# Norms of memory, cross-attention and first feed-forward: raw rows turned and split inside the preceding product, root mean square applied at eviction

## What is computed

```
mem_h = rms_norm(mem, mem_norm_g)
x = x + hybrid_mixer(rms_norm(x, mix_norm_g), ...)            # ends with @ w_mix_out
x = x + memory_cross_attention(rms_norm(x, xa_norm_g), mem_h, w_xq, w_xkv, w_xo)
x = x + conv_glu_ffn(rms_norm(x, ffn_norm_g), w_gate, w_up, ffn_conv_w, ffn_conv_b, w_down)
x = rms_norm(x, final_norm_g)

def rms_norm(x, g):
    return x * rsqrt(mean(x * x, axis=-1) + EPS) * g

def memory_cross_attention(h, mem_h, w_xq, w_xkv, w_xo):
    q = h @ w_xq
    kv = mem_h @ w_xkv          # keys: columns 0 to 2047, values: 2048 to 4095
    ...                          # 4 heads of 512, softmax over the 256 rows of memory
    return o @ w_xo
```

## Time and profile before

| | |
|---|---|
| median of 3 runs | 3050.98 us (3050.21 to 3056.83) |
| the profiled execution's own time | 3051.17 us |
| its span, first to last instruction | 3049.4 us |
| granted TensorE clock, mean | 0.961 of full speed |
| TensorE matmul busy | 2847.0 us, 93% |
| VectorE busy | 1822.8 us, 60% |
| ScalarE busy | 1300.3 us, 43% |
| moved by DMA | 579.27 MB, mean 190 GB/s |

### The profile page before, as it was taken

The page is one execution under the profiler, slowest core; times in us unless marked ns, Lnnn a source line. Parts: engine busy times, 40 slices in busy tenths (PEclk is TensorE's granted clock), DMA queues, the critical chain, the costliest instruction groups (busy, mean ns, idle before and its releaser), DMA issues.

```text
span 3049.4 us, 36718 instructions
## 1 busy us (share of the span) xinstructions
PE 2847.0 (93%) x13510; PEld 2411.1 (79%) x13510; DVE 1822.8 (60%) x2029; ACT 1300.3 (43%) x1519; POOL 181.1 (6%) x135
## 2 busy tenths in 40 slices
PE   7997899998988999999999979988888999999997
PEld 7996787787877888888888769777677888888885
DVE  6776647766747655544555477865466444444454
ACT  4444323444434555533444344334444434344442
POOL 0001440000000000000000000920000000000000
PEclk9998899999999999999999989988899999999998
DMA  8893008686838455555555558761273555555552
GB/s 292 294 322 106 0 28 289 240 282 209 280 106 275 147 184 179 179 193 187 185 179 193 176 209 298 234 233 56 71 260 112 195 189 180 192 193 180 193 180 97
DMA packets 291579, 579.27 MB, mean 190 GB/s; under 512 B 9040, under 2 KB 46064, under 8 KB 289936
## 3 DMA queue, kind: packets, MB, share of 16 engines
q1 hardware_dynamic: 289920, 565.03, 55.3%
q0 software_dynamic: 1552, 12.76, 1.1%
HBM read 575.66 MB, written 2.10 MB: 189 GB/s over the span
## 4 chain that ended last, share of the span: by engine, by line
PE 86%; DVE 8%; ACT 3%; issue 2%; DMA 1%; POOL 0%; DVEq 0%; SPq 0%; ACTq 0%; POOLq 0%
PE GP L812 25%; PE GP L814 25%; PE GP L813 25%; PE TA L788 2%; PE TB L439 2%; PE TB L788 1%; DVE wlo L1498 1%; DVE ada_acc L1486 1%; PE TA L1103 1%; DMA raw<-in_w_in 1%; PE GP L425 1%; ACT whi L1174 1%; DVE flat L1574 1%; PE GP L788 0%; PE TB L829 0%
## 5 line engine op out<-in xcount | busy, mean ns | idle before, releaser
L1498 DVE TENSOR_TENSOR wlo<-raw,whi 128x1024 fp32r<-128x1024 f32 (+2 forms) x904 | 1082.1, 1215 | 820.1 <-ACT whi L1174 808.3
L1174 ACT CAST whi<-raw 128x1024 fp32r<-128x1024 f32 (+2 forms) x904 | 921.4, 1030 | 1219.8 <-PE GP L814 1168.5
L812 PE MATMUL GP<-whi,hhi 128*128 128x512 f32 (+2 forms) x2752 | 1067.2, 388 | 30.1 <-DVE wlo L1498 26.8
L813 PE MATMUL GP<-wlo,hhi 128*128 128x512 f32 (+2 forms) x2752 | 1058.5, 385 | 0.0
L814 PE MATMUL GP<-whi,hlo 128*128 128x512 f32 (+2 forms) x2752 | 1058.2, 385 | 0.0
L812 PEld LDWEIGHTS GP<-whi,hhi 128*128 128x128 f32 x2752 | 520.5, 189 | 123.5 <-DVE wlo L1498 22.5
L814 PEld LDWEIGHTS GP<-whi,hlo 128*128 128x128 f32 x2752 | 519.9, 189 | 89.6
L813 PEld LDWEIGHTS GP<-wlo,hhi 128*128 128x128 f32 x2752 | 520.3, 189 | 88.0 <-issue 1.0
L1486 DVE SCALAR_TENSOR_TENSOR ada_acc<-raw,csig,ada_acc 128x512 f32<-128x512 f32 x360 | 284.6, 790 | 10.2
L812 PE MATMUL GP<-whi,f2hi 128*128 128x512 f32 x512 | 204.7, 400 | 0.0
L814 PE MATMUL GP<-whi,f2lo 128*128 128x512 f32 x512 | 202.8, 396 | 0.0
(11 more groups left out here) (370 smaller groups left out, 1899.2 us busy)
## 6 DMA issues: line engine op xcount, KB each, us to landing
raw<-in_w_up SPq DMA_DIRECT2D x108, 1024.0 KB, 5.2
raw<-in_w_down SPq DMA_DIRECT2D x108, 1024.0 KB, 5.1
raw<-in_w_ada SPq DMA_DIRECT2D x96, 1024.0 KB, 5.1
raw<-in_w_gate SPq DMA_DIRECT2D x44, 1024.0 KB, 5.1
raw<-in_w_in SPq DMA_DIRECT2D x48, 856.0 KB, 5.0
raw<-in_w_xkv SPq DMA_DIRECT2D x32, 1024.0 KB, 5.3
raw<-in_w_in SPq DMA_DIRECT2D x24, 1024.0 KB, 5.1
raw<-in_w_in SPq DMA_DIRECT2D x24, 864.0 KB, 4.8
```

What stands on the lines that cost most here:

```text
L812: pe.matmul(o, ahi[:, kt, t], whi[r][:, k, 0:q.width], start=first, stop=False)
L813: pe.matmul(o, ahi[:, kt, t], wlo[r][:, k, 0:q.width], start=False, stop=False)
L1174: nc.scalar.copy(whi[(2 * g + s) % NRING][:, :, 0:q.width], raw[j % NSLOT][:, 2 * s:2 * s + 2, 0:q.width])\
L1498: TTo(wlo[r][:, :, 0:q.width], raw[j % NSLOT][:, 2 * s:2 * s + 2, 0:q.width], whi[r][:, :, 0:q.width].bitcast(F32), ALU.subtract).then_inc ...
```

## The change

Rows are turned as they are, without the root mean square, and that factor is applied later, to the product's rows when they are evicted; it is the same for a whole row, so it may be moved behind the product. The gain, which belongs to columns, is applied when the turned columns are split. The steps:

- TensorE: `raw_turn(s, k)` turns 2 of the 16 groups of 128 columns (4 transposes) into one bank of `TA`. s = 0 is the memory, in mix_out; s = 1 is x, in xkvb; s = 2 is x again, in xo (k = 0 to 5) and in the first iteration of ffn1a (k = 6 and 7). xkv is now two phases, xkva with the keys and xkvb with the values.
- ScalarE: `raw_square` squares and sums the rows, `raw_root` takes the root of both halves of the tokens at once, `raw_upper` makes the upper part straight from PSUM, scaled by the gain.
- VectorE: `raw_mean`, `raw_scale` (the reciprocal) and `raw_lower`.
- Evictions of xkva, xkvb, xq, ffn1a and ffn1b: two scaled copies of 512 columns in place of one copy of 1024.
- The keys are turned inside xq (`key_turn`, 8 transposes behind each of its first four units) and copied there (`key_copy`).
- xkvb, xq, xo and mix_out have their last iteration written out, ffn1a its first.
- The split of x for the feed-forward goes to new tiles `bhi`, `blo`; `fhi` moves to the place of `hhi` and `hlo`. `fgb` lies where `bhi` and `blo` are, so POOL waits for ffn1b in place of down1b.

```diff
-          Phase("xkv", 4, 2, 4, 512, True), Phase("xq", 2, 2, 4, 512, True),
+          Phase("xkva", 2, 2, 4, 512, True), Phase("xkvb", 2, 2, 4, 512, True), Phase("xq", 2, 2, 4, 512, True),
...
+        def spot(v):
+
+            return (v // 8, v % 8 + 1) if v % 8 >= LEAD else (v // 8 - 1, v % 8 + 9)
...
             for e in range(2):
-                g.wait_ge(S(f"evac{e}"), 1 + PH["down1b"].ev1)
-            g.wait_ge(S("f1_lo"), 12)
+                g.wait_ge(S(f"evac{e}"), 1 + PH["ffn1b"].ev1)
             g.dma_start(fgb[:, :], A["final_norm_g"].partition_broadcast(P)).then_inc(S("fgb_in"), 16)
...
+            def raw_turn(s, k):
+                n = 8 * s + k
+                X = raws[s][0]
...
+                if n >= 2:
+                    pe.wait_ge(S("raw_lo"), n - 1)
+                for j in range(2):
+                    for h in range(NH):
+                        m = turn(raw_bank(n)[:, j * T + h * P:j * T + h * P + P], X[:, h, (2 * k + j) * P:(2 * k + j + 1) * P])
+                m.then_inc(S("raw_t"), 1)
...
-                    first=lambda: None, points={(0, 0, 1): dn_turn})
-            pe.wait_ge(S("evac1"), 1 + PH["mix_out"].ev1)
-            norm("mem")
-            product(PH["xkv"], hhi, hlo, lambda u: N("mem", "lo", 2 * u + 2))
-            for e in range(2):
-                pe.wait_ge(S(f"evac{e}"), 1 + PH["xkv"].ev1)
-            pe.wait_ge(S("ada_read"), 1 + PH["xkv"].ada1)
-            turn_in(pe, turn, "kx", kv, 0, 0)
-            norm("xa")
-            product(PH["xq"], hhi, hlo, lambda u: N("xa", "lo", 2 * u + 2))
+                    first=lambda: None, points={(0, 0, 1): dn_turn} | {unit_of(6 + k): lambda k=k: raw_turn(0, k) for k in range(8)})
+            product(PH["xkva"], mhi, mlo, lambda u: (S("raw_lo"), 2 * u + 2))
+            product(PH["xkvb"], mhi, mlo, lambda u: (S("raw_lo"), 8),
+                    first=lambda: None, points={unit_of(2 * k): lambda k=k: raw_turn(1, k) for k in range(8)})
...
+            product(PH["xq"], hhi, hlo, lambda u: (S("raw_lo"), 8 + 2 * u + 2),
+                    first=lambda: pe.wait_ge(S("raw_lo"), 16), points={unit_of(k): lambda k=k: key_turn(k) for k in range(4)})
...
-            product(PH["xo"], hhi, hlo, lambda u: N("xatt", "lo", 8))
-            norm("ffn")
+            product(PH["xo"], hhi, hlo, lambda u: N("xatt", "lo", 8), first=lambda: None,
+                    points={unit_of(v_): lambda k=k: raw_turn(2, k) for k, v_ in enumerate((6, 7, 10, 11, 14, 15))})
...
+            rest = product(PH["ffn1a"], bhi, blo, lambda u: (S("raw_lo"), 16 + 2 * u + 2), ffn1_mid(ba), ffn1_end(ba),
+                           points={(0, 0, 1): lambda: (raw_turn(2, 6), raw_turn(2, 7))})
...
+            def raw_upper(s, k):
+                n = 8 * s + k
+                act.wait_ge(S("raw_t"), n + 1)
+                _, g_, hi, _ = raws[s]
+                for j in range(2):
+                    m = nc.scalar.activation(hi[:, 2 * k + j, :], raw_bank(n)[:, j * T:j * T + T], ACT.Copy, scale=gains[:, g_, 2 * k + j:2 * k + j + 1])
+                m.then_inc(S("raw_hi"), 1)
...
+                            for h in range(NH):
+                                m = nc.scalar.activation(dst[:, h, bass.ds(col, q.width)], GP[:, 2 * e + h, 0:q.width], ACT.Copy,
+                                                         scale=scale_of[scale][:, h:h + 1])
...
+            phase(PH["mix_out"], hooked({6: lambda: raw_square(0, (0,)), 7: lambda: raw_square(0, (1,)), 11: lambda: raw_root(0)},
+                                        hooked(uppers(0, range(8, 16)))), peel=True)
+            phase(PH["xkva"], store(PH["xkva"], kv, scale=0))
+            phase(PH["xkvb"], hooked({3: lambda: raw_square(1, (0,)), 5: lambda: raw_square(1, (1,)), 9: lambda: raw_root(1)},
+                                     hooked(uppers(1, range(2, 18, 2)), store(PH["xkvb"], kv, base=2048, scale=0))), peel=True)
...
+            phase(PH["ffn1a"], ffn1(PH["ffn1a"], 0), head={3: [lambda it: raw_square(2)],
+                                                           4: [lambda it: (raw_upper(2, 6), raw_upper(2, 7), raw_root(2))]})
...
+            def raw_lower(s, k):
+                n = 8 * s + k
+                dve.wait_ge(S("raw_hi"), n + 1)
...
+                    m = nc.vector.scalar_tensor_tensor(lo[:, 2 * k + j, :], raw_bank(n)[:, j * T:j * T + T], gains[:, g_, 2 * k + j:2 * k + j + 1],
+                                                       hi[:, 2 * k + j, :].bitcast(F32), ALU.mult, ALU.subtract)
```

More of the change, by code:

```diff
@@ L211, in program @@
         STAGES, grown = {}, dict.fromkeys(("ss", "ms", "rt", "xn", "t", "f", "hi", "lo"), 0)
[L212 removed]
+        for n in ("mix", "fin", "pre2", "post0", "pf2", "post1"):
             STAGES[n] = ("norm", dict(grown))
@@ L601, in turn_in2_act, with raw_bank, hooked @@
                 m = nc.scalar.copy(dst[:, a:a + 4, :], v((TA, TB)[g % 2], T)).then_inc(N(nm_, "c")[0], 1)
[L603 to L606, removed]
+        xn_of = {"mix": xn, "pre2": xn_f, "pf2": None}
+        raws = [(memt, 2, mhi, mlo), (x, 1, hhi, hlo), (x, 3, bhi, blo)]
+        def raw_bank(n):
+            return TA[:, 512 * (n % 2):512 * (n % 2) + 512]
+        def spot(v):
+            return (v // 8, v % 8 + 1) if v % 8 >= LEAD else (v // 8 - 1, v % 8 + 9)
+        def hooked(table, more={}):
+            out = {at: list(fs) for at, fs in more.items()}
+            for v_, f in table.items():
+                t_, at = spot(v_)
+                out.setdefault(at, []).append(lambda it, t_=t_, f=f: f() if it == t_ else None)
+            return out
         ar = Arena(); ar.at = arena0 + 4 * NH * D
@@ L1193, in body, with phase @@
                         f(it)
-            def phase(q, hooks, peel=False, last={}, ahead=True):
+            def phase(q, hooks, peel=False, last={}, ahead=True, head={}):
                 i0 = order.index(q)
@@ L1200, in phase @@
                 m = q.n if same else q.n - 1
-                if m:
+                if head:
+                    body(q, 0, (q, 1), {at: hooks.get(at, []) + head.get(at, []) for at in hooks.keys() | head.keys()})
+                    with loop(act, m - 1) as i:
+                        body(q, i + 1, (q, i + 2), hooks)
+                elif m:
                     with loop(act, m) as it:
@@ L1519, in body, with phase @@
                     nc.vector.tensor_copy(mod[:, bass.ds(4 * (it + q.ada0), 4)], TB[:, 512:516]).then_inc(S("ada_read"), 1)
-            def phase(q, hooks, peel=False, links=0, last={}, ahead=True):
+            def phase(q, hooks, peel=False, links=0, last={}, ahead=True, head={}):
                 i0 = order.index(q)
@@ L1526, in phase @@
                 m = q.n if same else q.n - 1
-                if m:
+                if head:
+                    body(q, 0, (q, 1), {at: hooks.get(at, []) + head.get(at, []) for at in hooks.keys() | head.keys()})
+                    with loop(dve, m - 1) as i:
+                        with link.loop(i, m - 1, per):
+                            body(q, i + 1, (q, i + 2), hooks)
+                elif m:
                     with loop(dve, m) as it:
@@ L1742, in _ @@
                 TTo(hlo[:, 8:16, t], AB[0][hf], hhi[:, 8:16, t].bitcast(F32), ALU.subtract).then_inc(S("dn_lo"), 1)
-            phase(PH["mix_out"], add_to_x(PH["mix_out"]))
-            dve.wait_ge(S("mem_in"), 16)
-            norm("mem", memt, gains[:, 2, :])
-            phase(PH["xkv"], {})
-            norm("xa", x, gains[:, 1, :])
+            phase(PH["mix_out"], hooked({9: lambda: raw_mean(0), 12: lambda: raw_scale(0)},
+                                        hooked(lowers(0, range(8, 16)), add_to_x(PH["mix_out"]))), peel=True)
+            phase(PH["xkva"], {})
+            phase(PH["xkvb"], hooked({7: lambda: raw_mean(1), 11: lambda: raw_scale(1)}, hooked(lowers(1, range(2, 18, 2)))), peel=True)
             phase(PH["xq"], {})
@@ L1753, in _ @@
             attention_dve(dve, link, "xatt", cross_units())
-            phase(PH["xo"], add_to_x(PH["xo"]))
-            norm("ffn", x, gains[:, 3, :])
+            phase(PH["xo"], hooked(lowers(2, (8, 9, 12, 13, 16, 17)), add_to_x(PH["xo"])), peel=True)
             def ffn1(q, fb0):
```

97 lines of the change are left out of this document (75 added, 22 removed).

## The result

The changed kernel takes 3027.81 us (median of 4 runs, 3025.5 to 3033.43), the kernel before 3052.13 in the runs beside it (4 runs, 3050.21 to 3056.83). The ratio is 0.992, 95% interval 0.9908 to 0.9933: 24.3 us less, where 41.6 were forecast. The time lies outside the range, 8 us above its upper end.

What follows compares the result with a forecast made beforehand. TensorE, busy for 86% of the span, was taken as the bound. 3051.17 - 49.05 (norm stretches) + 14.9 (transposes) - 4.1 (final norm) - 3.3 (ffn1a) = 3009.6, forecast as 3009.5 us, range 3004 to 3020.

Steps and rivals of the forecast that it cites:

- what bounds the kernel now: Whole kernel: TensorE, 86% of the span, is the bound; nothing is paid back behind the three norm stretches.
- The stretches that go: Boundaries mix_out to xkv, xkv to xq, xo to ffn1a: norm stretches without products vanish, -49.05 us.
- The insertions: Transposes inside products on TensorE: 22 insertions of 4 at 0.48 us, 5 of 8 at 0.87, together +14.9 us.
- The rule of the Trainium skill: Opposing estimate for the 128 inserted transposes: about 275 ns each, 35.2 us in place of 14.9, not counting for full clock.
- ScalarE and VectorE keep pace: Splits in the changed products arrive in time, no cost: 3.1 us left at the fullest place, 1.4 in ffn1a's first iteration.
- The final norm: Before the final norm: POOL fetches gains fgb a phase earlier, so VectorE no longer waits for them, -4.1 us.
- ffn1a's loop: Table load at ffn1a's loop top goes, and with it TensorE's five waits of about 0.66 us, -3.3 us.
- The rivals: Five alternatives: some waits return 0.16, a side gain fails 0.08, full-record transposes 0.03, VectorE limits 0.03, time returns as transfers 0.02.
- The one on waits: Rival, chance 0.16: half the short insertions wait 0.5 us and ffn1a's first iteration lacks 2 us, +7.5, 3017.
- The list of what would show the prediction wrong: Signs in the changed profile: matmul or transpose released by a norm's low part, clock under 1.00, ada iterations longer than insertions explain.

Runs made afterwards that it cites:

- the kernel moved by 224: Changed kernel with mhi, mlo, bhi, blo, flo, f2hi and f2lo moved up by 224 bytes: 2995.3 us, ratio 0.9815.
- doubled: Changed kernel with each of the 128 transposes of raw rows and keys issued twice: 3043.52 us, ratio 0.9972.
- `flo` at 64 or 128: Changed kernel with the arena's start rounded up to 64 bytes (3026.85 us) or to 128 bytes (3024.34 us) instead of 32.
- the counter-test: Kernel before with hhi, hlo and all tiles allocated behind them pushed 32 bytes up, raw, ring and x staying: 3090.64 us, ratio 1.0136.
- the aligned one: Changed kernel with tile small shortened by 8 floats, so the arena starts 32 bytes earlier, a multiple of 256 from the ring: 2996.79 us, ratio 0.9818.
- the kernel before with the peeled loop: Kernel before with ScalarE's first iteration of ffn1a written out, nothing else: 3049.25 us, ratio 0.9991.
- the one with the arena at 128: Kernel before with its arena's start rounded up to 128 bytes instead of 32: 3050.16 us, ratio 1.0002.

## Why the prediction was wrong

**The step that failed** is in "what bounds the kernel now", and it is an omission: "Nothing is paid back behind them: the iteration of xkv behind the first boundary also has TensorE busy throughout". That was read from the kernel before, and it holds for what a stall leaves behind. But the change also moves the activations of xkv, ffn1a and ffn1b to other tiles, and the sum has no term for it: a product's own time was taken as unchanged ("the sums at an iteration's end 44.4 us apart in xkva"; they were 45.69). It wasn't. The new tiles stand 32 bytes off a multiple of 256 from the weights, and each triple costs 0.70 us in place of 0.68, 19.2 us for 960. Busy time hides this, since TensorE is 100% busy either way. The trace of the kernel before could have told it: its products from `fhi` were at 0.70 already, and were never compared with those from `hhi`.

**Point by point.**
- *The stretches that go*, 49.05 us: right. All three boundaries are at 0.81 us.
- *The insertions*, 0.48 us for 4 and 0.87 for 8: right. With the products' own price taken out, (47.27 - 44.44) / 6 = 0.47 us in mix_out and (46.38 - 44.45) / 4 = 0.48 in xkvb of the kernel moved by 224. Those of 8 in xq cost (48.10 - 44.44) / 4 = 0.91 in the changed kernel, which sums to 14.9 us or a little more.
- *The rule of the Trainium skill*, "TensorE: Matmul & The Clock Gate", Part 4 (PE-mode transpose), some 275 ns each and no full clock from them: the record still has 0.27 us, but 0.11 is what a transpose cost when doubled, and the granted clock stayed 1.00 with six insertions in the iteration.
- *ScalarE and VectorE keep pace*: right. In the trace of the changed kernel TensorE has no idle time from 471.42 us, inside mix_out's first iteration (there is a wait of 6.72 us for `wlo` in front of it; the kernel before has one of 6.82 at 465.29), to the turns of the queries at 835.56. The narrowest place, ffn1a's first iteration, was worked out to end its low parts 17.1 us behind xo's last unit. VectorE's timeline there:

```profile
988.05 1.65 DVE L1644 SCALAR_TENSOR_TENSOR blo<-TA,tab,bhi 128x256 fp32r<-128x256 f32 x4
989.70 0.17 DVE L1637 RECIPROCAL small<-small 128x2 f32<-128x2 f32 x1
```

  They end at 989.70, and xo's last unit at 972.68, where its turn starts: 17.0 us. TensorE began the unit that reads them at 991.67, 2.0 us later, where 1.4 of slack were forecast.
- *The final norm*, -4.1 us: 4.3 in the trace, 5.3 by medians.
- *ffn1a's loop*, -3.3 us: the mechanism is right and the size is too small. 3.2 us of waits are gone, but the stage gets 4.8 us shorter, since only idle time was charged; the medians, 2.4 apart, don't resolve it.
- *The rivals*: none of them came. The one on waits named 3017, and what it would have shown, waits at insertions, isn't there. The missing case was that a product without any wait gets slower. The list of what would show the prediction wrong did hold it: "ada iterations longer than their insertions explain".

The sum with the missing term is 3009.6 + 19.2 = 3028.8, and with 4.8 for ffn1a's loop 3027.3, against 3027.81. That it comes this close is in part luck: single executions of one kernel differ by 8 us.

## What to carry to other kernels

An edit that moves a tile changes the operands of every instruction that reads it: charge the instruction again by a row with that tile, and before trusting "unchanged" compare the distance from start to start of the same instruction with different tiles in the trace that is there already. When an engine is 100% busy in both kernels, look for a longer distance and not for a wait; the sums at an iteration's end showed it to 0.1 us. Judge a change of structure with the addresses held alike: here 32 bytes cost the kernel before 40 us, as much as the whole change was forecast to give. And charge a wait by the distance between starts, not by its idle time.

## What was not expected of the hardware

**The distance between operands.** An fp32r matmul of 128x512 starts 0.2267 us after the one before when its stationary tile lies a multiple of 256 bytes from its moving tile, and 0.2333 when the remainder is 32 or 64 (0.2326 at 128): 2.9%. These are means over hundreds of triples with no wait in them. It can be enough that the lower tile alone is off: in the changed kernel `fhi` lies at 98432 and `flo` in the arena at a remainder of 32, and down1's triples take 0.700; with `flo` at 64 or 128 they take 0.693. The Trainium skill, "SBUF — State Buffer", Who interferes with whom, gives TensorE two read ports, independent, one for the moving operand and one for the weight load, and says that it never waits on anyone. The runs here show that the addresses of the two together set its pace; that the two reads meet in the memory is what this suggests, and nothing here shows it. Narrower products can be read in the counter-test: triples of 428 columns took 0.58 us in both kernels, those of 432 went from 0.589 to 0.595. Other remainders, types and shapes were not tried.

**What stays open.** Why only some remainders cost, and why 428 columns don't, was not found out. The other open point is the delta-rule stage, a part of the mixer, which lies ahead of all changed work and varies from one execution to the next; by medians the tiles moved by 224 gave 32.5 us and by profiled spans 38.3, while the table above has what they gave in the part that they touch. In the profiled execution of the changed kernel that stage ran with a lower granted clock than in that of the aligned one, which has the same instructions there. Two stretches, the changed kernel first, the aligned changed kernel behind it:

```profile
340.00:380.00 40.00, 37.54 (x304) 36.61 (x302) 23.84 (x29) 9.22 (x13) 29.24 (x20) 0.91 0.00 0
446.50:462.80 16.30, 16.30 (x59) 12.04 (x60) 5.74 (x6) 1.22 (x2) 3.42 (x1) 0.76 0.32 120
```

```profile
340.00:380.00 40.00, 36.06 (x315) 35.00 (x314) 25.00 (x30) 9.35 (x15) 30.25 (x21) 1.00 0.00 0
446.50:462.80 16.30, 11.87 (x61) 9.83 (x59) 9.03 (x10) 5.50 (x8) 4.22 (x2) 0.98 0.21 76
```

In the one TensorE's granted clock is 0.91 and 0.76 of full speed, in the other 1.00 and 0.98. So mix_out ended its first iteration at 506.69 us, and not at 499.85 as before, of which the two insertions explain 1.0. It isn't the change: the kernel before with the peeled loop ended it at 507.87, the one with the arena at 128 at 498.14. Which executions get which was not found out, and single spans of this kernel should not be compared to better than some 10 us.
